# Expert matrices in a mixture-of-experts step: runs of 8 KB instead of 4 KB, and a matching column order for what meets them

## The chip, the cores and the metric

The kernel runs on one core of a Trainium2 chip. The metric is the device time of one execution in microseconds (us); lower is better. The core has TensorE (matmuls and transposes, PE in the profile), VectorE (DVE), ScalarE (ACT), GpSimd (POOL) and SyncE (SP, which here only issues DMAs). Sixteen DMA engines bring data from device memory (HBM) into on-chip memory (SBUF); matmuls write into eight banks of PSUM.

## The reference, cut to what matters

One layer of an encoder over 288 tokens (256 prompt, 32 sample) of width 1024, all in float32. After a first part (pooling, convolution, gates, output projection) each token goes to 4 of 32 experts:

```python
for e in range(N_EXPERTS):                      # 32
    gt = minimum(t @ exp_w_gate[e] + exp_b_gate[e], 7)
    up = clip(t @ exp_w_up[e] + exp_b_up[e], -7, 7)
    act = gt * sigmoid(1.702 * gt) * (up + 1.0)
    out = out + combine[:, e:e+1] * (act @ exp_w_down[e] + exp_b_down[e])
```

`t` is 288 x 1024 and each of the three matrices of an expert is 1024 x 1024 float32, 4 MB; the 32 experts are 403 MB.

## The kernel before

**Two parts.** The front part computes everything ahead of the experts and the routing. Then a loop runs over items: an item is one expert with up to 64 of its tokens, and an expert with more than 64 tokens has a second item with the same weights. In the profiled execution there are 33 items. Every engine runs the same loop with its own instructions, and semaphores order them.

**The ring.** Weights come in pieces of 1 MB into `ring`, 12 slots of 8 KB per partition. An expert is 12 pieces: 4 of the gate matrix, 4 of the up matrix, 4 of the down matrix, piece i in slot i. SP issues them in order (L376, in `expert`) and waits for each on `piece_used`, which PE counts up when it has finished with a slot. When a piece has landed, GpSimd's loop (L467) tells PE through `weights_ready`. A second item of the same expert loads nothing.

**Rows and partitions before.** Row `k*128 + p` of a matrix lies in partition p of block k, k from 0 to 7; a piece is two blocks, so each partition takes two runs of 4 KB, which lie 512 KB apart in HBM.

**One item on PE**, in this order: the bias rows (L1306) and the gate product (`product`, L1294); the scatter of the previous item's results back to two of the three token tiles (`scatter`, L1322); bias and the first half of the up product; scatter of the last token tile; the second half of the up product; the gather of the next item's tokens (`gather`, L1273, a matmul with a one-hot matrix into bank 0); four transposes of this item's activations (L1359, into bank 2); four transposes of the next item's tokens (`turn_tokens`, L1284, into bank 1); the down product, with transposes of a one-hot matrix in its middle (`turn_ohw`, L1371). A product is 8 blocks times 2 halves of the output columns; its left operand for block k is a slice of a transposed tile:

```python
def half_of(buf, k):
    return buf[:, P * (k % 4) + 64 * (k // 4):P * (k % 4) + 64 * (k // 4) + 64]
```

**What stands between the matmuls.** The gathered tokens are in bank 0 as 128 partitions (two halves of the width, 64 tokens each) by 512 columns. ACT copies them to `xg` (L623); PE's `turn_tokens` waits for that copy (`xg_ev`), transposes `xg` in four blocks of 128 columns, and ACT copies the result to `xgT` (L625), which the next item's products read. ACT's other work in an item is the sigmoid of the gate (L621), the copy of the turned one-hot matrix (L627) and of the item's result (L629). DVE clips the gate (L948), adds scattered results to `acc` (L927), clips the up product (L955), and forms the activations `acts` (L958); PE transposes `acts` (L1359), DVE copies the result to `actT` (L961), and the down product reads that. Before the loop the first item's tokens are copied the same way (L613, L615).

Of the kernel before, what the change touches and what calls it, by code (L numbers as in the profile page):

```python
# [21 lines left out]
ACT = mybir.ActivationFunctionType  # L22
AX = mybir.AxisListType.X

P = 128
# [52 lines left out]
def build(nc, x_prompt, x_sample, state_pool, state_conv, c_prompt, c_sample, norm1_g, norm2_g, final_g,  # L78
# [3 lines left out]
    with ExitStack() as ctx:  # L82
        def sb(name, shape, dt=F32):
            return ctx.enter_context(nc.sbuf_tensor(name, shape, dt))

        def sem(name):
            return ctx.enter_context(nc.semaphore(name))


        ring = sb("ring", [P, RING, SLOT])  # L90
# [37 lines left out]
        def view(start, *shape):  # L128
            n = 1
            for s in shape:  # L130
                n *= s
            a = arena[:, start:start + n]
            if len(shape) == 2:
                a = a.rearrange("p (a b) -> p a b", b=shape[1])
            return a
# [24 lines left out]
        xg = view(5376, HALF)  # L160
# [3 lines left out]
        gsig = view(512, HALF)  # L164
        ucl = view(1024, HALF)
        acts = view(1536, HALF)
# [12 lines left out]
        bank = [ctx.enter_context(nc.psum_tensor(f"bank{i}", [P, HALF], F32)) for i in range(8)]  # L179


        slot_ld = [sem(f"slot_ld{s}") for s in range(RING)]
# [90 lines left out]
        xg_ev = sem("xg_ev")  # L273
# [34 lines left out]
        poolw_v = pool_w[0].rearrange("g c o -> c g o")  # L308
        convw_v = conv_w_out[0].rearrange("(k p) n -> p k n", p=P)
        wout_v = w_out[0].rearrange("(k p) n -> p k n", p=P)  # L310
        wg_v = exp_w_gate[0].rearrange("e (k p) n -> e p k n", p=P)
        wu_v = exp_w_up[0].rearrange("e (k p) n -> e p k n", p=P)
        wd_v = exp_w_down[0].rearrange("e (k p) n -> e p k n", p=P)

        def front_piece(f):

            kind, a, b = FRONT[f]
            slot = ring[:, f % RING, :]
            if kind == "ada":
                return wada_v[b][:, 4 * HALF * a:4 * HALF * (a + 1)], slot  # L320
            if kind in ("in", "gate"):
                src = win_v if kind == "in" else gate_v
                return src[:, :, 256 * a:256 * (a + 1)], slot.rearrange("p (k n) -> p k n", k=KD)
            if kind == "pool":
                return poolw_v, slot[:, 0:D].rearrange("p (k n) -> p k n", k=CT)
            if kind == "conv":
                return convw_v[:, :, HALF * a:HALF * (a + 1)], slot.rearrange("p (k n) -> p k n", k=CT)
            return (wout_v[:, 4 * a:4 * a + 4, HALF * b:HALF * (b + 1)], slot.rearrange("p (k n) -> p k n", k=4))
# [32 lines left out]
        @block.sync  # L361
        def _(sp):
            sp.dma_start(x[:, 0:2, :], x_prompt[0].rearrange("(t p) d -> p t d", p=P)).then_inc(x_ld, 16)
            sp.dma_start(x[0:NS_TOK, 2, :], x_sample[0]).then_inc(x_ld, 16)
            for f in range(N_FRONT):
                if f >= RING:
                    sp.wait_ge(piece_used, f - RING + 1)
                src, dst = front_piece(f)
                sp.dma_start(dst, src).then_inc(slot_ld[f % RING], 16)

            def expert(e, last_use):

                for i in range(PIECES):
                    sp.wait_ge(piece_used, last_use(i))
                    w = (wg_v, wu_v, wd_v)[i // 4]
                    sp.dma_start(ring[:, i, :].rearrange("p (k n) -> p k n", k=2),  # L376
                                 w[e][:, 2 * (i % 4):2 * (i % 4) + 2, :]).then_inc(slot_ld[i], 16)

            expert(0, lambda i: max(f for f in range(N_FRONT) if f % RING == i) + 1)
            sp.wait_ge(base_ready, 1)  # L380
            with sp.Fori(1, E) as e:

                at = sp.value_load(base_i[0:1, bass.ds(e, 1)], min_val=1, max_val=MAX_ITEMS)
                expert(e, lambda i: at * PIECES + (F_END - PIECES + i + 1))
            sp.dma_start(fgb, final_g.rearrange("(a d) -> a d", a=1).broadcast_to([P, D])).then_inc(fg_ld, 16)
            for i, t in enumerate(LAST_ORDER):
                sp.wait_ge(y_ready, i + 1)
                dst = y_sample[0] if t == 2 else y_prompt[0, P * t:P * (t + 1), :]
                sp.dma_start(dst, ybuf[0:ROWS[t], t, :]).then_inc(stored, 16)
            sp.wait_ge(stored, 16 * (4 + TT))  # L390
# [80 lines left out]
        def _(act):  # L471
            a = nc.scalar
# [24 lines left out]
            for t in range(TT):  # L497
                r = ROWS[t]
# [87 lines left out]
            for i, t in enumerate(OUT_ORDER):  # L586
                r = ROWS[t]
# [22 lines left out]
            a.activation(ohwT, bank[1][:, 0:TT * P], ACT.Copy).then_inc(ohwT_ev, 1)  # L610

            act.wait_ge(xg_mm, 1)
            a.activation(xg, bank[0][:, :], ACT.Copy).then_inc(xg_ev, 1)  # L613
            act.wait_ge(xgT_mm, 1)
            a.activation(xgT, bank[1][:, :], ACT.Copy).then_inc(xgT_ev, 1)  # L615
            act.sem_inc(y_ev, 1)
# [2 lines left out]
            with act.Fori(0, items) as n:  # L619
                act.wait_ge(gate_read, n + 2)  # L620
                a.activation(gsig, gmin, ACT.Sigmoid, scale=ALPHA).then_inc(gsig_ready, 1)  # L621
                act.wait_ge(xg_mm, n + 2)
                a.activation(xg, bank[0][:, :], ACT.Copy).then_inc(xg_ev, 1)  # L623
                act.wait_ge(xgT_mm, n + 2)
                a.activation(xgT, bank[1][:, :], ACT.Copy).then_inc(xgT_ev, 1)  # L625
                act.wait_ge(ohwT_mm, n + 2)
                a.activation(ohwT, bank[1][:, 0:TT * P], ACT.Copy).then_inc(ohwT_ev, 1)  # L627
                act.wait_ge(y_mm, n + 1)
                a.activation(ysb, bank[5][:, :], ACT.Copy).then_inc(y_ev, 1)  # L629

            for i, t in enumerate(LAST_ORDER):
                r = ROWS[t]
# [9 lines left out]
        def _(dve):  # L642
            v = nc.vector
            n = [0]
# [26 lines left out]
            for t in range(TT):  # L671
                r = ROWS[t]
# [106 lines left out]
            for m in range(KD):  # L779
                dve.wait_ge(pm_mm, m + 1)  # L780
                v.scalar_tensor_tensor(out=merged[:, m, :], in0=bank[m % 4][:, 0:TOK],
                                       scalar=cols[:, C_PS + m:C_PS + m + 1], in1=gates[:, m, :],
# [21 lines left out]
            for i, t in enumerate(OUT_ORDER):  # L804
                r, gg = ROWS[t], t // 2
# [19 lines left out]
                if i == 0:  # L825
                    dve.wait_ge(spread_ld[1], 64)
                step(v.scalar_tensor_tensor(out=h2[0:r, t, :], in0=x[0:r, t, :], scalar=stat[0:r, 4 + t:5 + t],
                                            in1=a2b[0:r, gg, :], op0=ALU.mult, op1=ALU.mult))
# [64 lines left out]
            for m in range(2, MAX_ITEMS_E):  # L893
                step(v.scalar_tensor_tensor(out=rt[:, 2, 0, :], in0=rt[:, 1, 0, :], scalar=float(m * SLOTS),
                                            in1=rt[:, 2, 0, :], op0=ALU.is_gt, op1=ALU.add))
# [35 lines left out]
            with dve.Fori(0, items) as n_e:  # L931
                nxt = dve.value_load(owner_i[0:1, bass.ds(n_e + 1, 1)], min_val=0, max_val=E)

                dve.wait_ge(ohwT_mm, n_e + 1)
                for t in range(TT):
                    ins = v.tensor_scalar(ohw[:, t, :], both, item_col[:, 0, t:t + 1], item_col[:, 1, t:t + 1],  # L936
                                          ALU.is_equal, ALU.mult)
                ins.then_inc(ohw_ready, 1)

                dve.wait_ge(ohw_ready, n_e + 1)  # L940
                v.tensor_scalar(item_col[:, 0, :].unsqueeze(2), routed[:, 0, :, bass.ds(nxt, 1)],
                                first[:, bass.ds(n_e + 1, 1)], None, ALU.subtract)
                v.tensor_copy(item_col[:, 1, :].unsqueeze(2), routed[:, 1, :, bass.ds(nxt, 1)]).then_inc(col_ready, 1)
                dve.wait_ge(col_ready, n_e + 1)
                dve.wait_ge(xg_mm, n_e + 1)
                one_hot()
                dve.wait_ge(gate_done, n_e + 1)
                v.tensor_scalar(gmin, bank[3][:, :], LIMIT, None, ALU.min).then_inc(gate_read, 1)  # L948
                add_back((0, 2), n_e * 2 + 1)
                dve.wait_ge(gsig_ready, n_e + 1)  # L950
                dve.wait_ge(gate_read, n_e + 2)
                v.tensor_tensor(gsig, gmin, gsig, ALU.mult).then_inc(gs_ready, 1)
                add_back((1,), n_e * 2 + 2)
                dve.wait_ge(up_done, n_e + 1)
                v.tensor_scalar(ucl, bank[4][:, :], LIMIT, -LIMIT, ALU.min, ALU.max).then_inc(up_read, 1)  # L955
                dve.wait_ge(up_read, n_e + 2)
                dve.wait_ge(gs_ready, n_e + 1)
                v.scalar_tensor_tensor(out=acts, in0=ucl, scalar=1.0, in1=gsig,  # L958
                                       op0=ALU.add, op1=ALU.mult).then_inc(act_ready, 1)
                dve.wait_ge(actT_mm, n_e + 1)  # L960
                v.tensor_copy(actT, bank[2][:, :]).then_inc(actT_ev, 1)  # L961

                v.tensor_scalar(mine[:, :], part_no[:, :], owner[0:E, bass.ds(n_e + 1, 1)], None,
                                ALU.is_equal).then_inc(mine_ready, 1)
# [446 lines left out]
```

## Time and profile before

| what | value |
|---|---|
| median of 3 timed runs | 1296.8 us |
| lowest and highest | 1296.54 and 1300.01 us |
| span of the profiled execution, first to last instruction | 1297.5 us |
| PE busy in it | 1258.3 us, 97% |
| DVE busy | 457.0 us, 35% |
| ACT busy | 185.0 us, 14% |
| moved by DMA | 456.01 MB, mean 351 GB/s |

The span of the profiled execution is 0.7 us above the median of the timed runs, and no time of that execution other than its span is shown. PE's matmuls are pipelined and their ends are modelled, so its busy share says that it seldom waits, not that it is at its peak.

### The profile page before, as it was taken

To read this page: it belongs to the slowest core of one execution; us is meant where nothing else is said; L and a number is where in the kernel's file an instruction comes from. 1 tells how busy PE (TensorE), PEld (TensorE's weight loads), DVE (VectorE), ACT (ScalarE), POOL (GpSimd) and SP (SyncE) were. 2 spreads that over 40 slices of the span, in tenths; PEclk is the share of its full clock that TensorE was granted. 3 is DMA by queue.
4 is the path that set the end of the run, shared out by engine and by line. 5 is a ranking of instruction groups with operands and counts; after the bars stand their busy time and mean duration, and the time that the engine had idled before them with its cause. 6 is when DMAs were issued, how large, how long until landed. Compare 5 with 4: busy or idle time off the path is not lost.

```text
span 1297.5 us, 16426 instructions
## 1 busy us (share of the span) xinstructions
PE 1258.3 (97%) x5654; PEld 464.8 (36%) x5654; DVE 457.0 (35%) x1006; ACT 185.0 (14%) x295; POOL 38.0 (3%) x56
## 2 busy tenths in 40 slices
PE   5999999999999999999999999999999999999995
PEld 1676664533333333333333333333333333333331
DVE  2497235632223332322323222322222223333236
ACT  1111201211111111111111111111111111111112
POOL 1062000100000000000000000000000000000000
PEclk9999999899999999999999999999999999999998
DMA  9947654599999999999994699999999999999970
GB/s 355 372 168 293 246 212 135 198 367 409 405 402 408 407 403 408 407 405 405 404 406 195 240 390 409 406 403 406 404 404 407 406 406 408 403 407 406 404 300 36
DMA packets 129418, 456.01 MB, mean 351 GB/s; under 512 B 8377, under 2 KB 23285, under 8 KB 126331
## 3 DMA queue, kind: packets, MB, share of 16 engines
q1 hardware_dynamic: 126960, 452.23, 89.1%
q10 hardware_dynamic: 2443, 3.58, 0.9%
q8 instruction: 9, 0.15, 0.0%
q14 instruction: 6, 0.05, 0.0%
HBM read 454.38 MB, written 1.40 MB: 351 GB/s over the span
## 4 chain that ended last, share of the span: by engine, by line
PE 87%; DVE 6%; DMA 4%; ACT 2%; issue 1%; SPq 0%; POOLq 0%; DVEq 0%
PE bank L1294 53%; PE bank L1322 8%; PE bank L1273 6%; PE bank L1306 5%; DVE h L731 5%; PE bank L1112 3%; DMA ring<-in_exp_w_up 3%; PE bank L1189 2%; PE bank L1284 2%; ACT arena L623 1%; PE bank L1029 1%; DMA ring<-in_w_ada 1%; PE bank L1371 1%; PE bank L1083 1%; PE bank L1171 1%; PE bank L1016 1%
## 5 line engine op out<-in xcount | busy, mean ns | idle before, releaser
L1294 PE MATMUL bank<-ring,arena 128*64 128x512 f32 x3168 | 716.2, 597 | 3.1
L1294 PEld LDWEIGHTS bank<-ring,arena 128*64 128x64 f32 x3168 | 213.8, 136 | 452.1 <-issue 397.8
L927 DVE TENSOR_TENSOR arena<-arena,bank 128x512 f32<-128x512 f32 (+1 forms) x198 | 126.6, 680 | 126.8 <-PE bank L1322 126.3
L948 DVE TENSOR_SCALAR arena<-bank 128x512 f32<-128x512 f32 x33 | 22.8, 691 | 311.2 <-PE bank L1294 311.2
L1322 PE MATMUL bank<-arena 64*128 64x512 f32 (+1 forms) x396 | 106.8, 628 | 0.0
L1273 PE MATMUL bank<-h,arena 128*64 128x512 f32 x408 | 93.6, 593 | 0.0
L623 ACT ACTIVATE arena<-bank 128x512 f32<-128x512 f32 x33 | 19.7, 597 | 412.2 <-PE bank L1273 412.2
L936 DVE TENSOR_SCALAR arena<-slot_no,item_col 128x128 f32<-128x128 f32 x99 | 28.3, 343 | 134.8 <-PE bank L1371 132.9
L1306 PE MATMUL bank<-biases,mine 32*64 32x512 f32 x264 | 70.9, 613 | 0.0
L1112 PE MATMUL bank<-arena,ring 128*128 128x288 f32 x256 | 64.0, 408 | 0.0
L731 DVE SCALAR_TENSOR_TENSOR h<-h,dwc 128x318 f32<-128x318 f32 x120 | 61.9, 593 | 0.0
L1112 PEld LDWEIGHTS bank<-arena,ring 128*128 128x128 f32 x256 | 48.1, 190 | 16.3 <-issue 3.4
L621 ACT ACTIVATE arena<-arena 128x512 f32<-128x512 f32 x33 | 20.8, 629 | 227.3 <-DVE arena L948 227.3
L1322 PEld LDWEIGHTS bank<-arena 64*128 64x128 f32 (+1 forms) x396 | 24.5, 158 | 78.6 <-issue 78.6
L1273 PEld LDWEIGHTS bank<-h,arena 128*64 128x64 f32 x408 | 29.3, 138 | 59.3 <-issue 59.3
L955 DVE TENSOR_SCALAR arena<-bank 128x512 f32<-128x512 f32 x33 | 22.8, 692 | 75.9 <-PE bank L1294 75.9
L1083 PE MATMUL bank<-arena,ring 128*128 128x288 f32 x192 | 47.0, 407 | 0.0
L961 DVE COPY arena<-bank 128x512 f32<-128x512 f32 x33 | 22.8, 692 | 57.3 <-PE bank L1359 57.3
L621 ACT ACT_TABLE_LOAD x33 | 42.3, 1283 | 1.0 <-issue 0.4
L1083 PEld LDWEIGHTS bank<-arena,ring 128*128 128x128 f32 x192 | 36.4, 190 | 10.4 <-issue 0.5
L1029 PE MATMUL bank<-ring,cT 128*32 128x512 f32 x192 | 28.4, 708 | 7.2 <-DMA ring<-in_w_ada 7.2
L629 ACT ACTIVATE arena<-bank 128x512 f32<-128x512 f32 x33 | 19.7, 597 | 102.4 <-PE bank L1294 102.4
(221 smaller groups left out, 586.0 us busy)
## 6 DMA issues: line engine op xcount, KB each, us to landing
ring<-in_exp_w_gate SPq DMA_DIRECT2D x128, 1024.0 KB, 8.5
ring<-in_exp_w_up SPq DMA_DIRECT2D x128, 1024.0 KB, 8.3
ring<-in_exp_w_down SPq DMA_DIRECT2D x128, 1024.0 KB, 6.9
ring<-in_w_ada SPq DMA_DIRECT2D x24, 1024.0 KB, 10.7
ring<-in_gate_w SPq DMA_DIRECT2D x8, 1024.0 KB, 5.5
ring<-in_w_in SPq DMA_DIRECT2D x6, 1024.0 KB, 13.4
ring<-in_w_out SPq DMA_DIRECT2D x4, 1024.0 KB, 6.4
ring<-in_conv_w_out SPq DMA_DIRECT2D x2, 1024.0 KB, 8.4
```

Of the source, the lines that this page charges most:

```text
L621: a.activation(gsig, gmin, ACT.Sigmoid, scale=ALPHA).then_inc(gsig_ready, 1)
L623: a.activation(xg, bank[0][:, :], ACT.Copy).then_inc(xg_ev, 1)
L731: ins = v.scalar_tensor_tensor(out=yc[:, c, :], in0=uc_ext[:, c, k:k + CW], scalar=tap, in1=yc[:, c, :], op0=ALU.mult, op1=ALU.add)
L927: ins = v.tensor_tensor(acc[0:r, t, cs], acc[0:r, t, cs], src, ALU.add)
L936: ins = v.tensor_scalar(ohw[:, t, :], both, item_col[:, 0, t:t + 1], item_col[:, 1, t:t + 1], ALU.is_equal, ALU.mult)
L1029: ins = mm(out[32 * j:32 * j + 32, :], cT[:, k, :], ring[:, f % RING, HALF * j:HALF * (j + 1)], start=(k == 0), stop=(k == KD - 1), skip_g ...
L1083: ins = mm(bank[n % 4][:, 0:TOK], w[:, k, P * (n % 2):P * (n % 2 + 1)], hT[:, k, :], start=(k == 0), stop=(k == KD - 1))
L1112: ins = mm(bank[n % 4][:, 0:TOK], w[:, k, P * (n % 2):P * (n % 2 + 1)], hT[:, k, :], start=(k == 0), stop=(k == KD - 1))
L1273: ins = mm(bank[0][64 * hh:64 * hh + 64, :], oh[:, t, :], h2[:, t, HALF * hh:HALF * (hh + 1)], start=(t == 0), stop=(t == TT - 1), skip_gr ...
L1294: ins = mm(out[64 * hh:64 * hh + 64, :], lhs(k), ring[:, s, D * (k % 2) + HALF * hh:D * (k % 2) + HALF * (hh + 1)], start=(done is y_mm an ...
L1306: ins = mm(out[64 * hh:64 * hh + 64, :], mine[:, :], bias_table[:, row, HALF * hh:HALF * (hh + 1)], start=True, stop=False, skip_group_che ...
L1322: ins = mm(out, ohwT[64 * hh:64 * hh + 64, P * t:P * t + ROWS[t]], ysb[64 * hh:64 * hh + 64, :], start=True, stop=True, skip_group_check=True)
```

## The change

Row `h*512 + 4*p + 2*q + r` of an expert's matrix now lies in partition p; h and q pick the piece, r the half of the slot. So each partition of a piece takes one run of 8 KB (two neighbouring rows), and the runs of neighbouring partitions lie 16 KB apart. A product contracts over the 1024 rows, so what it multiplies must come in the same order: block j of half h must hold columns `512*h + 4*p + j` instead of `512*h + 128*j + p`. The new order is made where the tile that is transposed is written: column 4*q + j of the source goes to column 128*j + q of `xg` and of `acts`. The source is read in its order (`in_order`), and the writes step through the destination (`by_row`) by 128 columns, 512 bytes, for each of four elements, and then come back to the next column. The number of instructions, of DMAs and of bytes is the same, and no wait is added or taken away.

```diff
-        wg_v = exp_w_gate[0].rearrange("e (k p) n -> e p k n", p=P)
-        wu_v = exp_w_up[0].rearrange("e (k p) n -> e p k n", p=P)
-        wd_v = exp_w_down[0].rearrange("e (k p) n -> e p k n", p=P)
+        rows_of = "e (h p q r) n -> e p h q (r n)"
+        wg_v = exp_w_gate[0].rearrange(rows_of, h=2, q=2, r=2)
+        wu_v = exp_w_up[0].rearrange(rows_of, h=2, q=2, r=2)
+        wd_v = exp_w_down[0].rearrange(rows_of, h=2, q=2, r=2)
+        def by_row(ap):
+            return ap.rearrange("p (j q) -> p q j", j=4)
+        def in_order(ap):
+            return ap.rearrange("p (q j) -> p q j", j=4)
...
-                    sp.dma_start(ring[:, i, :].rearrange("p (k n) -> p k n", k=2),
-                                 w[e][:, 2 * (i % 4):2 * (i % 4) + 2, :]).then_inc(slot_ld[i], 16)
+                    sp.dma_start(ring[:, i, :], w[e][:, i % 4 // 2, i % 2, :]).then_inc(slot_ld[i], 16)
...
-            a.activation(xg, bank[0][:, :], ACT.Copy).then_inc(xg_ev, 1)
+            a.activation(by_row(xg), in_order(bank[0][:, :]), ACT.Copy).then_inc(xg_ev, 1)
...
-                v.scalar_tensor_tensor(out=acts, in0=ucl, scalar=1.0, in1=gsig,
+                v.scalar_tensor_tensor(out=by_row(acts), in0=in_order(ucl), scalar=1.0, in1=in_order(gsig),
                                        op0=ALU.add, op1=ALU.mult).then_inc(act_ready, 1)
```

The ACT edit stands twice in the code: ahead of the loop (L613) and in it (L623).

## Rows read from the trace of the kernel before

**Rows 1.** The page: busy time by engine, then the span in 40 slices.

```profile
PE 1258.3 (97%) x5654; PEld 464.8 (36%) x5654; DVE 457.0 (35%) x1006; ACT 185.0 (14%) x295; POOL 38.0 (3%) x56
...
DMA  9947654599999999999994699999999999999970
GB/s 355 372 168 293 246 212 135 198 367 409 405 402 408 407 403 408 407 405 405 404 406 195 240 390 409 406 403 406 404 404 407 406 406 408 403 407 406 404 300 36
```

**Rows 2.** The chain, 500 to 820 us: first pieces of items (start, us, what).

```profile
504.84 7.02 PE bank L1294 x32
535.87 7.02 PE bank L1294 x32
...
691.03 7.02 PE bank L1294 x32
722.07 7.02 PE bank L1294 x32
```

**Rows 3.** Busy by stretch: us, PE busy, PEclk, DMA share, GB/s.

```profile
12.00:26.00 14.00, 10.19 (x40) 1.00 1.03 408
504.84:535.87 31.03, 30.83 (x141) 1.00 1.02 406
700.00:722.00 22.00, 21.80 (x102) 1.00 0.00 0
```

**Rows 4.** The timeline, 525 to 528 us: start, us, engine, line, work, idle before.

```profile
525.63 0.66 PE L1359 MATMUL bank<-ident,arena 128*128 128x128 f32 x4
525.75 0.60 ACT L623 ACTIVATE arena<-bank 128x512 f32<-128x512 f32 x1 [12.49 <-PE bank L1273]
526.32 0.69 DVE L961 COPY arena<-bank 128x512 f32<-128x512 f32 x1 [1.74 <-PE bank L1359]
526.39 0.42 PEld L1284 LDWEIGHTS bank<-ident,arena 128*128 128x128 f32 x4 [0.34 <-ACT arena L623]
526.39 0.66 PE L1284 MATMUL bank<-ident,arena 128*128 128x128 f32 x4
527.09 0.60 ACT L625 ACTIVATE arena<-bank 128x512 f32<-128x512 f32 x1 [0.75 <-PE bank L1284]
527.15 1.08 PE L1294 MATMUL bank<-ring,arena 128*64 128x512 f32 x4
```

**Rows 5.** The timeline, rest of the same item.

```profile
506.89 6.55 SPq L376 DMA_DIRECT2D ring<-in_exp_w_gate  x4
523.90 0.69 DVE L958 SCALAR_TENSOR_TENSOR arena<-arena 128x512 f32<-128x512 f32 x1
530.73 0.55 PE L1371 MATMUL bank<-ident,arena 128*128 128x128 f32 x3
```

**Rows 6.** Waits of the whole span: us in total, times, longest us.

```profile
PEld bank L1294 <- issue: 397.8, 1324, 0.8
PEld bank L1294 <- POOLq L467: 54.2, 95, 0.8
PEld bank L1284 <- ACT arena L623: 11.4, 33, 0.3
```

**Rows 7.** Groups of instructions by shape: count, busy us, mean ns, idle before.

```profile
L623 ACT ACTIVATE arena<-bank 128x512 f32<-128x512 f32 x33 | 19.7, 597 | 412.2 <-PE bank L1273 412.2
L627 ACT ACTIVATE arena<-bank 128x384 f32<-128x384 f32 x33 | 16.2, 491 | 119.8 <-PE bank L1371 119.8
L667 DVE TENSOR_TENSOR cT<-c_cols,csig 128x16 f32<-128x16 f32 x1 | 0.2, 178 | 0.3 <-ACT csig L486 0.3
L901 DVE TENSOR_TENSOR base<-base 128x16 f32<-128x16 f32 x1 | 0.2, 169 | 0.0
```

**Rows 8.** Line L376, SP's issues of expert pieces, and the time to landing.

```profile
L376 SPq DMA_DIRECT2D ring<-in_exp_w_gate x128: 367/373/579, 175.6 to 1226.8; - x128
DMA to landing us min/median/max: 4.7/7.9/15.6
```

**Rows 9.** Busy by stretch in the front part, pieces in short runs.

```profile
38.00:40.00 2.00, 2.00 (x8) 1.00 1.10 348
```

More of the change, by code:

```diff
@@ L622, in _ @@
                 act.wait_ge(xg_mm, n + 2)
-                a.activation(xg, bank[0][:, :], ACT.Copy).then_inc(xg_ev, 1)
+                a.activation(by_row(xg), in_order(bank[0][:, :]), ACT.Copy).then_inc(xg_ev, 1)
                 act.wait_ge(xgT_mm, n + 2)
```

## The prediction

> **What bounds the kernel now.** I read the page first: PE is busy for 97% of the span, and the DMA engines look full too, at about 406 GB/s in most slices of the expert loop [rows 1]. Two resources at their limit at once would make a change of the transfers worth something, so the first question is which of them sets the pace. Two slices answer it: there DMA falls to 195 and 240 GB/s while PE does not let up. This is the second item of one expert, for which nothing is loaded.
>
> The chain that ended last gives the pace. It enters a gate product, the first piece of work of an item, at 504.84 and again at 535.87 us: 31.03 us per item. The item in which nothing is loaded goes from 691.03 to 722.07, which is 31.04 us [rows 2]. The busy time by stretch shows that DMA moved 0 GB/s from 700 to 722 us, with PE at 21.80 of 22.00 us, and 406 GB/s in the loaded item, with PE at 30.83 of 31.03 [rows 3]. So an item takes as long with no transfer at all as with 12.58 MB of them. The loop is PE's, at a granted clock of 1.00, and DMA follows: 12.58 MB in 31.03 us is 405.5 GB/s, the rate that the page shows, because PE frees slots at that pace. 33 items (the count of L623 in [rows 7]) of 31.03 us are 1024 of the span's 1297.5 us.
>
> Is there any slack for a late piece? SP reissues the first gate slot at 506.89 us [rows 5] and the next item reads it at 535.87 [rows 2], 29.0 us later; pieces land a median of 7.9 us after their issue, 15.6 at most [rows 8]. The slack is 29.0 - 7.9 = 21.1 us. The waits table names GpSimd's message about landed weights (POOLq L467) 95 times before a weight load, 54.2 us together; but that is 0.57 us each and never over 0.8, and the same gap is named "issue" 1324 times, up to the same 0.8 [rows 6]. It is the gap of a wait instruction, not of missing data.
>
> Last I looked at where PE does wait inside an item. The timeline around 526 us shows one place: the four transposes of activations (L1359) end at 525.63 + 0.66 = 526.29; ACT's copy of the gathered tokens (L623) runs from 525.75 to 526.35; the transposes of the tokens (L1284) start at 526.39 and end at 527.05, and the down product starts at 527.15 [rows 4]. The waits table has this wait 33 times, 11.4 us in all [rows 6]. PE is through with everything else when it needs L623, so that copy is on the path that sets the end, with no slack: each 0.1 us more on it is 0.1 us more per item, 3.3 us in all.
>
> **The change, part by part.**
>
> *The transfers.* As many DMAs and bytes as before. Their size on SP's queue is no issue: an issue takes 0.373 us [rows 8], 12 of them 4.5 us of an item's 31. What rate have runs of 8 KB? The front part's first pieces (`w_ada`, 2048 columns of one row per partition) are such runs; from 12 to 26 us, when almost nothing else flows, the engines moved 408 GB/s, against 406 in the expert loop at runs of 4 KB [rows 3]. The least favourable neighbour is runs of 1 KB, 348 GB/s [rows 9]. I take 408, the row with the same length of run. Either way a faster transfer is worth 0 here, and the cover is the 21.1 us of slack together with the no-load item. A slower one costs nothing either until the slack is used up (worked out below). The first expert's gate pieces are issued from 175.6 us on [rows 8], and the first item begins 8 items before 504.84, at 256.6; they aren't waited for.
>
> *The copy to `xg` (L623), on the path.* Its duration is 0.597 us for 512 columns. A copy of 384 columns (L627) takes 0.491 [rows 7]: 0.106 us for 128 columns, 0.83 ns per column. What the new order costs the trace does not show, since no ACT instruction of it writes with such steps. I bound it. Below: 0, if a write to any place takes its one turn; nothing in the change can make the copy shorter, so there is no gain to allow for. Above: a write that never has its neighbour right behind it may need a second turn, 512 x 0.83 ns = 0.424 us, or a third, 0.849 us. The only hint comes from DVE: L667 reads both its sources with a step of 8 columns, 16 elements, and takes 178 ns, where L901 with 16 elements in a row takes 169 [rows 7]. That is 9 ns more, 0.56 ns per element, about half of a turn, and for 512 elements 0.29 us. It is small, it concerns reads, and instructions this short hide part of their cost; but it is not zero. I take one more turn, 0.424 us, between 0 and 0.849 and nearest to that hint.
>
> L667 points the same way as a rule of the Trainium skill, which speaks against this change: Vector Engine (DVE) Microarchitecture Reference, "Measured stream behaviour on trn2", says that a port keeps its full rate only while elements come as at least two adjacent 4-byte words, and gives 1.71 ns per column instead of 1.054 where the destination hops at every element, and 2.50 for steps of 24 words. By that page, an estimate for VectorE alone, L623 would grow by 512 x 0.66 = 0.34 us (11 us in 33 items) or, as for small steps, by 0.74 us (24 us); no row here shows either for ACT.
>
> The wait that follows grows by the same amount: L1284 would start at 526.81 and the down product at 527.57. Behind L623 in ACT's queue is L625, which waits for L1284 and ends at 528.1 instead of 527.69; its first reader is `turn_ohw`, whose transposes start at 530.73 [rows 5], still 2.6 us later. 33 x 0.424 = 14.0 us. The copy ahead of the loop (L613) is covered in part by matmuls that only keep PE busy; 0.2 us. DVE's L961 ends at 527.01 [rows 4] and no longer comes close to deciding.
>
> *The activations (L958), beside the path.* DVE runs it from 523.90 to 524.59 [rows 5]; the transposes that read it start at 525.63, behind the gather [rows 4]. Slack 1.04 us. A second turn per element is 512 x 1.04 ns = 0.53 us and is hidden by the gather; only a third, 1.07 us, would show, by 0.03. Its two sources are read in their order. I count 0.
>
> *Sum.* 1297.5 + 14.0 + 0.2 = 1311.7 in terms of the profiled span, which lies 0.7 above the median: 1311.0 us.
>
> **The rivals.**
>
> *Hopping writes are free (the other side: not slower).* If ACT takes any address in its one turn, nothing on PE's path changes, and the gain of the transfers is hidden: 1296.8 us, up to the 1300 that one of the three runs shows. For it speaks that the hint of L667 is only 9 ns; against it, that the hint exists. It decides below 0.118 us more per copy (0.3% of 1296.8 is 3.9 us, which is about what a measurement of this kernel can tell from no change; over 33 items 0.118 us).
>
> *A third turn.* L623 grows by 0.849 us and L958 by up to 1.07: 33 x 0.85 = 28, 1325 us.
>
> *DMA becomes the bound.* Pieces now are 8 KB of every 16 KB of address, in each DMA the same half. An item's pieces take 12.58 MB / rate. After the no-load item 17 items load without a break, so the 21.1 us of slack last while an item's transfer takes under 31.03 + 21.1/17 = 32.3 us: from 390 GB/s down this decides. At 348 GB/s [rows 9] a transfer takes 36.1 us, 5.1 more than the item: 17 x 5.1 - 21 = 66 after the no-load item and 14 x 5.1 - 21 = 50 before it, 1413 us with no ACT cost. Against it stands 408 GB/s for runs of 8 KB [rows 3], though those lie 24 KB apart and not 16. The Trainium skill (DMA: Bandwidth & Descriptors, "Latency and other measured facts") has slow copies at pitches of large powers of two, from 512 KB; no run here shows what it would say of 16 KB.
>
> *Faster.* PE would have to be waiting for pieces after all. If the 54.2 us put down to POOLq were data [rows 6], some of it could come back, at most 54: 1243 us. The no-load item, which can wait for no landing and takes 31.04 us, speaks against it.
>
> **How the numbers follow.** One more turn, or something between 0.25 and 0.6 us per copy: 0.50. A third turn: 0.15. Free or under 0.118 us: 0.26. DMA as bound: 0.04. Faster: 0.05. The predicted time is that of the likeliest case, 1311 us, whose own range is 1305 to 1317 (0.25 to 0.6 us in 33 items). The range that holds 8 in 10 must take in the free case below and the third turn above, since leaving out either with the tails leaves too much out: 1296 to 1326. Slower by over 0.3%: 0.50 + 0.15 + 0.04 = 0.69; within: 0.26; faster: 0.05.
>
> **What the profile after would show.** L623 at about 1.02 us (0.60 if writes are free), the wait of L1284 for it at 0.77 us instead of 0.34, and an item of 31.45 us with or without loads. L958 at about 1.2 us, with the start of L1359 unmoved within the item. L625, L961 and L1294 as before. The DMA rate in the loop at 12.58 MB / 31.45 us = 400 GB/s, following PE down, and landing times near 8 us; packets larger. It would be wrong if L623 kept 0.60 us, if DVE's copy suffered far more than ACT's (over 1.04 us more moves the path to L958), or if items with loads were longer than the one without.

## The result, and the profile after

The changed kernel takes 1306.56 us (median of 19 runs), the kernel before beside it 1299.25 us (19 runs). One of the 19 runs of the changed kernel, of 1321.78 us, was a slow one and is left out of the ratio. The ratio of after to before is 1.0058, 95% interval [1.0038, 1.0078]: slower by about 7.5 us, between 5 and 10. The profiled executions have spans of 1304.3 and 1297.5 us.

From the page of the kernel after: busy time by engine, what the DMA engines moved in each of the 40 slices, and their packets; last the packets of the kernel before.

```profile
PE 1252.8 (96%) x5654; PEld 461.9 (35%) x5654; DVE 469.4 (36%) x1006; ACT 200.5 (15%) x295; POOL 38.0 (3%) x56
...
GB/s 355 373 174 280 261 196 156 213 384 399 405 398 406 404 402 402 403 403 402 407 403 148 262 400 401 397 402 399 399 404 404 402 405 404 403 399 405 403 289 36
DMA packets 80266, 456.01 MB, mean 350 GB/s; under 512 B 8377, under 2 KB 23285, under 8 KB 28027
```

```profile
DMA packets 129418, 456.01 MB, mean 351 GB/s; under 512 B 8377, under 2 KB 23285, under 8 KB 126331
```

ACT is busy 15.5 us longer and DVE 12.4 us, while PE is busy 5.5 us less [rows 1]. The longer runs are there: with the same bytes, 28027 of 80266 packets are under 8 KB, where 126331 of 129418 were. But the rate in the loop is a little lower than before, not higher: a loaded item moves the same bytes in a longer time, so the transfers follow PE.

The chain of the kernel after, from 500 to 820 us, at the start of four gate products, and the groups of instructions by shape for the two edited copies (these lines stand seven further down in the changed kernel):

```profile
504.38 7.02 PE bank L1301 x32
535.70 7.02 PE bank L1301 x32
...
692.30 7.02 PE bank L1301 x32
723.62 7.02 PE bank L1301 x32
```

```profile
L630 ACT ACTIVATE arena<-bank 128x512 f32<-128x512 f32 x33 | 34.7, 1051 | 412.1 <-PE bank L1280 412.1
...
L965 DVE SCALAR_TENSOR_TENSOR arena<-arena 128x512 f32<-128x512 f32 x33 | 35.3, 1071 | 1.1
```

An item takes 31.32 us, where it took 31.03 [rows 2], and again the item in which nothing is loaded (692.30 to 723.62) takes as long as the others. ACT's copy of the tokens went from 597 to 1051 ns [rows 7], DVE's write of the activations to 1071 ns from the 0.69 us of [rows 5]. The first is 0.454 us more, yet the item is only 0.288 us longer. The timeline of the kernel after around that copy shows where the rest is (start, us, engine, line, work, and in brackets the idle time before):

```profile
525.18 0.66 PE L1366 MATMUL bank<-ident,arena 128*128 128x128 f32 x4
525.29 1.05 ACT L630 ACTIVATE arena<-bank 128x512 f32<-128x512 f32 x1 [12.49 <-PE bank L1280]
525.87 0.69 DVE L968 COPY arena<-bank 128x512 f32<-128x512 f32 x1 [1.35 <-PE bank L1366]
...
526.40 0.66 PE L1291 MATMUL bank<-ident,arena 128*128 128x128 f32 x4 [0.56 <-ACT arena L630]
...
526.98 0.20 PEld L1301 LDWEIGHTS bank<-ring,arena 128*64 128x64 f32 x4 [0.17 <-POOLq L474]
526.98 1.51 PE L1301 MATMUL bank<-ring,arena 128*64 128x512 f32 x6
```

And one line of the kernel before that [rows 4] does not have, the weight load with which the down product begins:

```profile
527.14 0.20 PEld L1294 LDWEIGHTS bank<-ring,arena 128*64 128x64 f32 x4 [0.33 <-POOLq L467]
```

PE now stands idle for 0.56 us ahead of the token transposes. But the down product follows them without a gap: it starts at 526.98, 0.58 us after the start of the transposes, where it was 0.76 before (526.39 to 527.15 in [rows 4]). The idle time ahead of its first weight load shrank from 0.33 to 0.17 us. The profile puts both down to GpSimd's message, so its name for a releaser did not give this wait away; its length did. What had gone unnoticed in [rows 4] is DVE's copy L961. It ended at 527.01, and the down product, which waits for it too, began 0.14 us later. Here that copy (L968) ends at 526.56 and decides nothing.

33 items of 0.288 us are 9.5 us. The spans differ by 6.8, because the profiled execution of before came later out of the front part: there ACT began the copy of the first item's result at 286.65 us, after the change at 284.19. The window from 225 to 250 us, before and after (us, PE busy, granted clock, DMA share, GB/s):

```profile
225.00:250.00 25.00, 23.92 (x115) 0.80 0.73 271
```

```profile
225.00:250.00 25.00, 23.52 (x126) 0.93 0.72 262
```

PE's granted clock there, in the routing with its short bursts of matmuls, was 0.80 in one execution and 0.93 in the other, each a mean of stretches at 2.4 GHz and at 1.2 GHz. The front part varies like this from execution to execution, for every kernel below; the length of an item does not. So the experiments are read by the item first and by the ratio second.

Much of the front part's share drops out between executions with the same granted clock, as a mean over the whole execution. At 0.991, three executions of the changed kernel took 1309.43 to 1309.64 us, and eleven of the kernel before, timed beside the experiments, 1299.57 to 1300.74, median 1299.96: 9.6 us between the medians. At 0.986, two took 1315.24 and 1315.44 us against a median of 1305.6 in twelve (1304.85 to 1307.98): 9.7 us. Both agree with the 9.5 us of the loop. The 7.3 us between the medians of all runs mixes executions with different front parts.

### The profile page after: what moved, and what is told of

It reads as the page before. It is cut to its first block, busy times and chain, and to the rows that moved or that the text cites. A ratio compares the mean times of both kernels' runs of the same rounds, so it can differ in the third digit from the quotient of the medians.

```text
span 1304.3 us, 16426 instructions
## 1 busy us (share of the span) xinstructions
PE 1252.8 (96%) x5654; PEld 461.9 (35%) x5654; DVE 469.4 (36%) x1006; ACT 200.5 (15%) x295; POOL 38.0 (3%) x56
## 2 busy tenths in 40 slices
DMA packets 80266, 456.01 MB, mean 350 GB/s; under 512 B 8377, under 2 KB 23285, under 8 KB 28027
## 4 chain that ended last, share of the span: by engine, by line
PE 89%; DVE 6%; ACT 3%; DMA 1%; issue 0%; SPq 0%; DVEq 0%
PE bank L1301 54%; PE bank L1329 8%; PE bank L1280 7%; PE bank L1313 5%; DVE h L738 5%; PE bank L1119 3%; ACT arena L630 3%; PE bank L1196 2%; PE bank L1291 2%; PE bank L1036 1%; DMA ring<-in_w_ada 1%; PE bank L1378 1%; PE bank L1090 1%; PE bank L1178 1%; PE bank L1023 1%; PE bank L1055 1%
## 5 line engine op out<-in xcount | busy, mean ns | idle before, releaser
L630 ACT ACTIVATE arena<-bank 128x512 f32<-128x512 f32 x33 | 34.7, 1051 | 412.1 <-PE bank L1280 412.1
L1291 PE MATMUL bank<-ident,arena 128*128 128x128 f32 x136 | 22.3, 286 | 18.8 <-ACT arena L630 18.6
L968 DVE COPY arena<-bank 128x512 f32<-128x512 f32 x33 | 22.8, 691 | 44.7 <-PE bank L1366 44.7
L965 DVE SCALAR_TENSOR_TENSOR arena<-arena 128x512 f32<-128x512 f32 x33 | 35.3, 1071 | 1.1
```

The lines of the kernel that those rows point to most:

```text
L630: a.activation(by_row(xg), in_order(bank[0][:, :]), ACT.Copy).then_inc(xg_ev, 1)
L965: v.scalar_tensor_tensor(out=by_row(acts), in0=in_order(ucl), scalar=1.0, in1=in_order(gsig), op0=ALU.add, op1=ALU.mult).then_inc(act_read ...
L1291: ins = tr(bank[1][:, P * j:P * (j + 1)], xg[:, P * j:P * (j + 1)], ident[:, :])
```

## The experiments

The item is worked out in each trace as the time from the first to the last of 33 copies of an item's result (L629 before, L636 after), over 32. In the two runs with half a product the items differ, and the steady ones are given. The intervals of e2, e3, e8, e9 and e10 rest on 4 runs each. "Tokens" is ACT's copy to `xg`, "activations" DVE's write of `acts`, mean ns.

| run | tokens | activations | item, us | ratio to before, 95% |
|---|---|---|---|---|
| before | 597 | 692 | 31.03 | |
| after | 1051 | 1071 | 31.32 | 1.0058 [1.0038, 1.0078] |
| e1_runs_only | 597 | 692 | 31.03 | 1.0009 [0.9989, 1.0028] |
| e2_order_only | 1050 | 1068 | 31.32 | 1.013 [1.008, 1.0179] |
| e3_act_order_only | 1050 | 692 | 31.32 | 1.0108 [1.0049, 1.0167] |
| e4_dve_order_only | 597 | 1067 | 31.03 | 1.0019 [0.9993, 1.0045] |
| e5_split_copy | 598 | 691 | 30.87 | 0.9983 [0.9947, 1.0019] |
| e6_pe_reads_steps | 598 | 692 | 31.12 | 1.004 [1.0003, 1.0076] |
| e7_engines_read_steps | 597 | 1103 | 31.03 | 1.001 [0.9974, 1.0047] |
| e8_half_product_4k | 597 | 692 | 30.72 | 0.9546 [0.948, 0.9612] |
| e9_half_product_8k | 1051 | 1069 | 29.83 | 0.9379 [0.931, 0.9449] |
| e10_cover_4k | 597 | 691 | 30.40 | 0.9844 [0.9773, 0.9914] |
| e11_cover_8k | 1066 | 1072 | 30.71 | 0.992 [0.9896, 0.9945] |
| e12_read_steps_cover | 597 | 1103 | 30.40 | 0.9843 [0.9806, 0.988] |

### The change taken apart: e1 to e4

e1 takes the DMA edit alone:

```diff
-            a.activation(by_row(xg), in_order(bank[0][:, :]), ACT.Copy).then_inc(xg_ev, 1)
+            a.activation(xg, bank[0][:, :], ACT.Copy).then_inc(xg_ev, 1)
...
-                v.scalar_tensor_tensor(out=by_row(acts), in0=in_order(ucl), scalar=1.0, in1=in_order(gsig),
+                v.scalar_tensor_tensor(out=acts, in0=ucl, scalar=1.0, in1=gsig,
```

> Runs of 8 KB alone: the expert matrices come as in the changed kernel, the gathered tokens and the activations stay in the old column order, so the products pair rows and columns of different numbers (the work is the same, the values are not). If PE sets the pace and the transfers are hidden: an item of 31.03 us as before, ratio to before 1.000. If the longer runs gave something back in the changed kernel (the rival by which the whole cost of the copies was partly repaid by faster transfers): an item under 31.03 us, about 30.87, ratio 0.996. If they cost something: over 31.03.

The item is 31.03 us and the ratio 1.0009 [0.9989, 1.0028]: the longer runs alone change nothing.

e2 is the reverse: the kernel before with both edited copies, and runs of 4 KB.

```diff
-            a.activation(xg, bank[0][:, :], ACT.Copy).then_inc(xg_ev, 1)
+            a.activation(by_row(xg), in_order(bank[0][:, :]), ACT.Copy).then_inc(xg_ev, 1)
...
-                v.scalar_tensor_tensor(out=acts, in0=ucl, scalar=1.0, in1=gsig,
+                v.scalar_tensor_tensor(out=by_row(acts), in0=in_order(ucl), scalar=1.0, in1=in_order(gsig),
```

> The new column order alone, on both copies, with the expert matrices in runs of 4 KB as before (rows and columns of different numbers are paired, as in the run with the runs alone). If all of the loss is the copy of the gathered tokens: an item of 31.32 us, as in the changed kernel, ratio 1.007. If the transfers had repaid part of it: up to 31.03 + 0.45 = 31.48 us, ratio 1.011.

31.32 us, the item of the changed kernel: the longer runs give nothing back there either. Its ratio, 1.013 [1.008, 1.0179] from 4 runs, lies above the 1.0073 that 33 times 0.288 us make. The loop does not explain that. In the profiled executions of this table with whole products the copy of the first item's result begins anywhere from 279.1 us (e4) to 298.0 us (e5), and from the end of the last such copy to the end of the span all take 17.2 to 17.3 us. So what differs in them beyond the items lies ahead of the loop's first result. Which part of it made e2's four runs long was not taken apart.

e3 makes the first of these two edits alone, e4 the second alone.

```diff
# e3, twice
-            a.activation(xg, bank[0][:, :], ACT.Copy).then_inc(xg_ev, 1)
+            a.activation(by_row(xg), in_order(bank[0][:, :]), ACT.Copy).then_inc(xg_ev, 1)
# e4
-                v.scalar_tensor_tensor(out=acts, in0=ucl, scalar=1.0, in1=gsig,
+                v.scalar_tensor_tensor(out=by_row(acts), in0=in_order(ucl), scalar=1.0, in1=in_order(gsig),
```

> The new order on ScalarE's copy of the tokens only, matrices and activations as before (rows and columns of different numbers are paired for the gate and up products). My theory: this copy at 1.05 us is the whole loss, item 31.32 us, ratio 1.007. Rival, that VectorE's slower write of the activations is part of it: item between 31.03 and 31.32.

> The new order on VectorE's write of the activations only (rows and columns of different numbers are paired for the down product). My theory: 1.07 us instead of 0.69, inside a slack of 1.04 us, so item 31.03 us and ratio 1.000. Rival: it moves the transposes of the activations and the copy behind them, item over 31.03 us by up to 0.38, ratio up to 1.010.

e3 has the whole loss, 31.32 us; e4 has none, 31.03 us, though its write takes 1067 ns. The loss per item is ACT's copy and nothing else. e3's ratio, again from 4 runs, lies above 1.0073 too, but its interval holds it.

### Where 0.165 us of the copy went: e5

The kernel before, with DVE's copy of the turned activations in two halves; the down product begins after the first.

```diff
-                v.tensor_copy(actT, bank[2][:, :]).then_inc(actT_ev, 1)
+                v.tensor_copy(actT[:, 0:256], bank[2][:, 0:256]).then_inc(actT_first, 1)
+                v.tensor_copy(actT[:, 256:512], bank[2][:, 256:512]).then_inc(actT_ev, 1)
...
                 for k in range(KD):
+                    if done is y_mm and k == 2:
+                        pe.wait_ge(actT_ev, n_i + 2)
...
-                pe.wait_ge(actT_ev, n + 2)
+                pe.wait_ge(actT_first, n + 1)
```

> The kernel before, with VectorE's copy of the turned activations (0.69 us) made as two copies of 256 columns; the first two blocks of the down product wait for the first one only. Theory A: the copy of the tokens had 0.16 us of slack in the kernel before, because the down product there waited for VectorE's copy of the turned activations (ended 527.01, product at 527.15) and not for the transposes of the tokens. Then this kernel's down product starts 0.1 to 0.16 us earlier: item about 30.9 us, ratio 0.996. Theory B: the 0.16 us is something else (a gap that any wait leaves); item 31.03 us, ratio 1.000.

30.87 us, 0.165 less than before, and 0.454 - 0.165 = 0.289 us, against the 0.288 that the item of the changed kernel grew by. Theory A holds. In the timeline of e5 the first half of the copy ends at 443.92 + 0.42 = 444.34, the transposes of the tokens start at 443.99, and the product starts 0.59 us after them, with 0.17 us of idle time ahead of its weight load as in the changed kernel:

```profile
443.92 0.42 DVE L962 COPY arena<-bank 128x256 f32<-128x256 f32 x1 [1.74 <-PE bank L1363]
...
444.58 0.20 PEld L1298 LDWEIGHTS bank<-ring,arena 128*64 128x64 f32 x4 [0.17 <-issue]
```

The ratio (0.9983 [0.9947, 1.0019]) can't confirm 5 us; the item does.

### The same order made elsewhere: e6 and e7

e6 copies in a row and lets PE read in steps; e7 lets ACT and DVE read in steps and write in a row. Both compute the whole layer.

```diff
+        def stepped(ap):
+            return ap.rearrange("p (q j) -> p j q", j=4)
# e6
-                    ins = tr(bank[1][:, P * j:P * (j + 1)], xg[:, P * j:P * (j + 1)], ident[:, :])
+                    ins = tr(bank[1][:, P * j:P * (j + 1)], stepped(xg)[:, j, :], ident[:, :])
# e7
-            a.activation(by_row(xg), in_order(bank[0][:, :]), ACT.Copy).then_inc(xg_ev, 1)
+            a.activation(xg.rearrange("p (j q) -> p j q", j=4), stepped(bank[0][:, :]), ACT.Copy).then_inc(xg_ev, 1)
```

> The changed kernel with both copies writing in a row as before (0.60 and 0.69 us) and PE's eight transposes reading the copied tiles with a step of 4 columns (16 bytes) instead. If TensorE's read takes any step at full rate: item 31.03 us, ratio 1.000 to before. If a stepped read costs it twice the time (transposes of 0.66 us become 1.1 to 1.3): item up to 32.0 us, ratio 1.03.

> The changed kernel with the new order made on the reading side of the same two instructions: they write in a row and read with a step of 4 columns (16 bytes), ScalarE from PSUM, VectorE from SBUF. If only writes with steps are slow: 0.60 and 0.69 us, item 31.03 us, ratio 1.000. If a stepped read costs the same as a stepped write: 1.05 us, item 31.32 us, ratio 1.007. VectorE has two stepped sources: up to 1.2 us, past the slack of 1.04 if over 1.7.

ACT pays nothing for the stepped read. A read of PSUM with a step of 16 bytes takes the same 597 ns as one in a row:

```profile
L633 ACT ACTIVATE arena<-bank 128x512 f32<-128x512 f32 x33 | 19.7, 597 | 411.6 <-PE bank L1283 411.6
...
L968 DVE SCALAR_TENSOR_TENSOR arena<-arena 128x512 f32<-128x512 f32 x33 | 36.4, 1103 | 1.1
```

With its two reads of SBUF in steps DVE's instruction takes 1103 ns, about as much as with its one stepped write (1071); that stays hidden. ACT's read differs from its write in three things, the side, the memory (PSUM, not SBUF) and the step (16 bytes, not 512); which of them makes it free is not shown, and DVE's case speaks against the side alone. The item is 31.03 us: the change with runs of 8 KB and no loss. In e6 four transposes take 0.75 us instead of 0.66, their weight loads 209 ns each instead of 141, and the item 31.12 us: my upper guess of twice the time was far off.

### Transfers as the bound: e8 and e9

The kernels before and after, with only every second block of a product computed; all pieces are still loaded.

```diff
-                    for hh in range(2):
+                    for hh in range(2) if k % 2 == 0 else ():
...
-                                 start=(done is y_mm and k == 0), stop=(done is y_mm and k == KD - 1) or k == KD - 1,
+                                 start=(done is y_mm and k == 0), stop=k == KD - 2,
```

> The kernel before, with only every second block of each product computed (the other row block of each piece is loaded and left out), so PE's item shrinks by 10.7 us to about 20 and the transfers set the pace. The item is then 12.58 MB at the engines' own rate: about 30.6 us at 411 GB/s for runs of 4 KB, ratio 0.985 or so.

> The changed kernel with the same half of each product left out. If runs of 8 KB move at the rate of 4 KB: the same item as in the run with half the product and 4 KB, about 30.6 us. If longer runs are faster (fewer packets): under 30.2 us. If the stretch of 8 KB in every 16 KB is slower: over 31 us. PE's copies don't matter at this pace.

The shortest items, around the one in which nothing is loaded, find their pieces landed and take 20.73 us in e8 and 21.02 in e9: that is PE's own pace. The steady ones take about 10 and 9 us longer, at a DMA share above 1. Windows of 200 us in the loop (us, PE busy, granted clock, DMA share, GB/s), first e8, then e9:

```profile
800.00:1000.00 200.00, 159.43 (x609) 0.90 1.03 410
```

```profile
800.00:1000.00 200.00, 160.86 (x619) 0.90 1.01 422
```

With 4 KB the steady item is 30.72 us, with 8 KB 29.83: 12.583 MB in these times are 409.6 and 421.8 GB/s. The medians are 1239.14 and 1222.26 us. So longer runs are faster, by 3% of an item, once PE does not set the pace. e8's item is as expected, its ratio of 0.9546 is not (0.985): five items, near the start and around the item without loads, took only 20.7 to 25.7 us, which the expectation left out. I had expected no difference from the 408 GB/s of [rows 3]. That stretch of the front part is not a clean row for runs of 8 KB: of its 1507 packets 792 were under 512 B, and a second queue moved 0.17 of the 5.71 MB and took 5.9% of the engines' time. How much of the rate this cost is not shown.

### A cover for the copy: e10, e11, e12

The transposes of the one-hot matrix move out of the down product to between the two other groups of transposes, into bank 3:

```diff
                 ins.then_inc(actT_mm, 1)
+                pe.wait_ge(ohw_ready, n + 1)
+                pe.wait_ge(gate_read, n + 2)
+                for t in range(TT):
+                    ins = tr(bank[3][:, P * t:P * (t + 1)], ohw[:, t, :], ident[:, :])
+                ins.then_inc(ohwT_mm, 1)
                 turn_tokens(n + 1)
...
-                product(bank[5], lambda k: half_of(actT, k), n, 8, y_mm, turn_ohw)
+                product(bank[5], lambda k: half_of(actT, k), n, 8, y_mm)
```

ACT copies that result before `xgT`, and PE waits for that copy ahead of the next gate product. e10 is this on the kernel before, e11 on the changed one, e12 on e7.

> The changed kernel with one step moved: the three transposes of the one-hot matrix (0.48 us), before in the middle of the down product, stand between the transposes of the activations and those of the tokens, in another bank, so PE works while ScalarE copies the tokens. If the loss is PE's wait for that copy (0.56 us idle ahead of the token transposes), it goes: the item is 31.32 us less about 0.5, near 30.8 us, under that of the kernel before, ratio 0.993. If the loss is elsewhere: item 31.3 us.

> The kernel before with the transposes of the one-hot matrix moved between those of the activations and those of the tokens, as in the changed kernel with that cover. Theory: the same item as there within 0.1 us, near 30.7 to 30.8 us, ratio 0.992, since the slower copy is hidden in one and absent in the other. If the slower copy still shows there by 0.1 us or more, the cover of 0.48 us is too short for 1.05 us.

> Both findings together, complete and with runs of 8 KB: the new order made on the reading side (ScalarE's copy of the tokens at 0.60 us, VectorE's write of the activations at 1.10 us inside its slack), and the transposes of the one-hot matrix moved into the wait for the copy. If the two add up as the single runs say: an item of 30.40 us, as with the cover and 4 KB, ratio 0.984; if VectorE's 1.10 us now shows, because less lies ahead of the transposes of the activations: up to 30.8 us, ratio 0.993.

e11's item falls from 31.32 to 30.71 us, under that of the kernel before. But e10 has 30.40, and the 0.31 us between them, where I had expected 0.1 at most, say that 0.48 us of work cannot hide all of the slow copy. e11's timeline shows what is left, 0.25 us of idle PE; e10's has no such wait. Why e10 gains 0.63 us over the kernel before, where 0.2 to 0.3 was expected, was not taken apart.

```profile
440.07 1.07 ACT L630 ACTIVATE arena<-bank 128x512 f32<-128x512 f32 x1 [12.49 <-PE bank L1280]
440.45 0.49 PE L1372 MATMUL bank<-ident,arena 128*128 128x128 f32 x3
...
441.19 0.66 PE L1291 MATMUL bank<-ident,arena 128*128 128x128 f32 x4 [0.25 <-ACT arena L630]
```

```profile
429.39 0.60 ACT L623 ACTIVATE arena<-bank 128x512 f32<-128x512 f32 x1 [12.49 <-PE bank L1273]
...
430.09 0.60 PE L1284 MATMUL bank<-ident,arena 128*128 128x128 f32 x4
```

e12 takes the copy at 597 ns and the cover together: 30.40 us per item, median 1276.26 us, ratio 0.9843 [0.9806, 0.988], faster than both kernels. Its 8 KB runs are not what makes it so, since e10 with 4 KB has the same item. What they give is room. A piece lands a median of 11.2 us after its issue in e10 and 8.2 us in e12. An item of 30.40 us is already shorter than the 30.72 that 4 KB runs need in e8; e10 lives on the lead of the ring, by an estimate from these two 0.32 us per item, about 5 us in the 17 items after the one without loads, inside the 21.1 us of slack. A PE item a good deal shorter would need the longer runs. That step was not tried.

## Why the prediction came out as it did

**What bounds the kernel.** PE sets the pace, transfers are hidden: shown. e1 is 31.03 us with the longer runs alone, and the item without loads is as long as the others in both kernels. The gaps put down to GpSimd are not missing data, as I said, but not all of them are only those of a wait instruction: the 0.33 us ahead of the down product held 0.16 us of waiting for L961.

**The rate of 8 KB runs.** Wrong in size, without effect here: 421.8 against 409.6 GB/s, not the same (e8, e9). The row behind the forecast of 408 was a mixed one, in which not "almost nothing else" flowed. The rival with DMA as the bound is out by a wide margin, and that with a gain needs a kernel in which PE is not the bound.

**One more turn per element on ACT.** Forecast 0.424 us, measured 0.454 (597 to 1051 ns). Right in the copy that pays and nearly in the size; free writes and a third turn are both out. That the cost is one more turn is not shown: 0.89 ns per column is near ACT's 0.83, but on DVE it is 0.379 us instead of up to 0.53, or 0.74 ns per column against the 1.04 that I took for a turn there. The choice of a whole turn for ACT rested on a hint from DVE's reads, so how near it came is luck in part. The wait of the token transposes' weight load was forecast at 0.77 us and is 0.80 (26.4 us in 33 items). By the Trainium skill (Vector Engine (DVE) Microarchitecture Reference, "Measured stream behaviour on trn2"), a destination which hops by 4 KiB at every element costs 1.71 ns per column instead of 1.054. For VectorE the trace nearly agrees, with hops of 512 bytes: an estimate of 0.34 us from that page, 0.375 measured in e4.

**"On the path, with no slack."** This is the term that was mis-sized: 14.0 us, measured 33 x 0.288 = 9.5. The slack of 0.165 us per item, 5.4 us in all, had been put at nothing; the copy itself was 0.03 us dearer than forecast, 1.0 us in all. In [rows 4] I read the 0.10 us between the end of the token transposes and the down product as nothing, and wrote that L961 "no longer comes close to deciding". Before the change it did decide, and it gave L623 0.165 us of room. e5 shows it by removing L961's share. An item of 31.45 us was forecast, and it is 31.32.

**Activations beside the path.** Right: e4 leaves the item at 31.03 us.

**The total.** Forecast 1311.0 us against a median before of 1296.8, so 14.2 more; measured 7.3 more between medians, 7.5 by the ratio. The loop's 9.5 us lie inside the ratio's interval of 5 to 10 us, and executions with the same granted clock differ by 9.6 and 9.7. The rest is the front part, whose length varies from execution to execution by more than that. That the forecast of the time itself is only 4.4 us off is luck in part: the kernel before was 2.5 us slower beside this result than in the three runs that the forecast started from.

## What to carry to other kernels

Before costing a longer instruction at full price, follow it to the next start that it feeds and list everything else that this start waits for: one that ends within 0.2 us of it may have been setting that start. The name of a releaser in the profile need not tell, as the down product's 0.33 us put down to GpSimd did not; comparing the idle time with that of the same instruction elsewhere does. When an order must be changed on the way through an engine, try both sides of the instruction: here ACT's stepped read of PSUM was free and its stepped write to SBUF was not, while DVE paid on both. And a resource that looks full may only be following the one that sets the pace; make the other one faster in an experiment, as e8 and e9 do, to see what the first can do.

## What the runs showed of the hardware that was not expected

- ACT reading PSUM float32 with a step of 16 bytes and writing in a row: 597 ns for 512 columns, the same as in a row (e7). Writing SBUF with a step of 512 bytes at every element: 1051 ns (after).
- DVE writing SBUF with that step: 1071 ns instead of 692 (after). With both sources read from SBUF with a step of 16 bytes and a write in a row: 1103 ns (e7).
- PE's transposes reading with a step of 16 bytes: weight loads of 209 ns instead of 141, 0.09 us more for four transposes (e6).
- Loads of 1 MB as 128 runs of 8 KB: 421.8 GB/s (e9); as 256 runs of 4 KB: 409.6 GB/s (e8), with a DMA share above 1 in both. SP's issue of one went from 373 to 333 ns (before and after).
